# A position bias table fetched in four groups of heads, and a sigmoid that changes places in the last feed-forward

## The reference

```python
rel = kj - BLOCK - qi
bias = rel_bias[t5_bucket(rel)].astype(jnp.float32)
bias = jnp.transpose(bias, (2, 0, 1)).reshape(N_KV_HEADS, G, 1, BLOCK, 3 * BLOCK)
...
scores = jnp.where(valid, scores + bias, NEG_INF)
```

```python
u = causal_dwconv(h2 @ w_up[l], conv_w[l], conv_b[l])
a, v = jnp.split(u, 2, axis=-1)
x = x + gt2 * ((jax.nn.silu(a) * v) @ w_down[l])
```

## Time and profile before

| | |
|---|---|
| median of 3 runs | 1354.23 us (1352.77 to 1354.25) |
| the profiled execution, its own time | 1350.6 us |
| its span, first to last instruction | 1348.8 us |
| PE busy | 1314.8 us |
| DVE busy | 1054.6 us |
| ACT busy | 698.5 us |
| POOL busy | 42.7 us |
| mean granted TensorE clock | 0.995 |
| bytes moved | 262.00 MB, mean 194 GB/s |

### The profile page before, as it was taken

The page is one execution under the profiler, slowest core; times in us unless marked ns, Lnnn a source line. Parts: engine busy times, 40 slices in busy tenths (PEclk is TensorE's granted clock), DMA queues, the critical chain, the costliest instruction groups (busy, mean ns, idle before and its releaser), DMA issues.

```text
span 1348.8 us, 22597 instructions
## 1 busy us (share of the span) xinstructions
PE 1314.8 (97%) x8928; PEld 1197.0 (89%) x8928; DVE 1054.6 (78%) x1814; ACT 698.5 (52%) x1124; POOL 42.7 (3%) x80
## 2 busy tenths in 40 slices
PE   6999999999999999999999999999999998999998
PEld 6999999998888889999999988888879876888886
DVE  4588668786778785787687776788899888688888
ACT  5454554444445454555544354454457566655553
POOL 1000000000000000000000000000010000000000
PEclk9999999999999999999999999999999998999999
DMA  8965435564777654544445745777634504345551
GB/s 264 230 239 185 176 127 217 188 219 157 256 277 285 257 188 157 183 162 156 143 155 220 249 188 199 273 283 290 236 108 172 220 32 145 115 163 207 197 190 61
DMA packets 42147, 262.00 MB, mean 194 GB/s; under 512 B 5229, under 2 KB 5613, under 8 KB 14782
## 3 DMA queue, kind: packets, MB, share of 16 engines
q1 hardware_dynamic: 32688, 227.28, 47.3%
q0 software_dynamic: 9264, 33.24, 7.4%
q10 hardware_dynamic: 94, 0.07, 0.0%
HBM read 258.99 MB, written 1.58 MB: 193 GB/s over the span
## 4 chain that ended last, share of the span: by engine, by line
PE 82%; DVE 10%; DMA 4%; ACT 2%; issue 1%; SPq 0%; DVEq 0%; ACTq 0%
PE psum L726 21%; PE psum L746 15%; PE psum L843 11%; PE psum L732 11%; PE psum L752 8%; PE psum L791 4%; DMA ring<-stream 3%; DVE split L1811 3%; PE psum L798 2%; PE psum L817 2%; PE psum L903 1%; PE psum L893 1%; PE psum L881 1%; DVE arena L1804 1%; PE psum L1012 1%
## 5 line engine op out<-in xcount | busy, mean ns | idle before, releaser
L1811 DVE TENSOR_TENSOR split<-ring,split 128x1024 fp32r<-128x1024 f32 x406 | 480.0, 1220 | 77.4 <-ACT split L1320 76.1
L1320 ACT CAST split<-ring 128x1024 fp32r<-128x1024 f32 x405 | 405.7, 1049 | 170.1 <-PE psum L732 74.4
L726 PE MATMUL psum<-h,split 128*128 128x256 f32 x2176 | 273.4, 283 | 1.0 <-ACT split L1320 1.0
L726 PEld LDWEIGHTS psum<-h,split 128*128 128x128 f32 x2176 | 265.7, 192 | 2.7 <-issue 1.9
L746 PE MATMUL psum<-h,split 128*128 128x512 f32 x960 | 229.0, 390 | 0.7 <-ACT split L1320 0.7
L746 PEld LDWEIGHTS psum<-h,split 128*128 128x128 f32 x960 | 177.7, 188 | 36.4 <-DVE arena L2632 1.1
L843 PE MATMUL psum<-split,feed 128*128 128x512 f32 x792 | 186.1, 391 | 1.3 <-DVE feed L1811 0.7
L843 PEld LDWEIGHTS psum<-split,feed 128*128 128x128 f32 x792 | 146.6, 188 | 31.7 <-DVE split L1811 1.5
L732 PE MATMUL psum<-h,split 128*128 128x256 f32 x1088 | 142.0, 283 | 0.2 <-DVE split L1811 0.2
L732 PEld LDWEIGHTS psum<-h,split 128*128 128x128 f32 x1088 | 135.6, 192 | 0.4 <-DVE split L1811 0.4
L752 PEld LDWEIGHTS psum<-h,split 128*128 128x128 f32 x960 | 123.3, 191 | 4.8
(11 more groups left out here) (328 smaller groups left out, 1389.2 us busy)
## 6 DMA issues: line engine op xcount, KB each, us to landing
ring<-stream SPq DMA_DIRECT2D x213, 1024.0 KB, 4.9
arena<-ada POOLq DMA_DIRECT2D x48, 512.0 KB, 5.3
arena<-bias_by_distance POOLq DMA_DIRECT2D x8, 384.0 KB, 29.7
gain<-norm_rows POOLq DMA_DIRECT2D x4, 512.0 KB, 6.3
x<-x_in SPq DMA_DIRECT2D x2, 512.0 KB, 4.8
ring<-stream SPq DMA_DIRECT2D x2, 512.0 KB, 7.2
gain<-mod_rows POOLq DMA_DIRECT2D x2, 512.0 KB, 4.1
out<-x SPq DMA_DIRECT2D x4, 256.0 KB, 2.0
```

Of the source, the lines that this page charges most:

```text
L726: pe.matmul(to[m], w[0][:, at + k, cols[m]], rhs[:, part, at + k, :], start=m == parts[0] and k + part == 0, stop=False)
L1320: act.copy(split_of(x)[:, 0, n], ring[:, AT[x] % RING, n]).then_inc(wh_ready, 1)
L1811: return dve.tensor_tensor(out_, value, high.bitcast(F32), ALU.subtract)
```

## The change

The bias fetch is cut into four groups of four heads, each of eight transfers of 96 KB, with a semaphore of its own. Group 0 is issued where all was issued before. Group 1 waits until (kd, 1) is done, group 2 until (c, 1) is done, `c_row` as before until (c, 2) is done, group 3 until (x, 3) is done, and the tables of the second block until (wa, 1) is done, which also holds back `gain`. `softmax_in` waits in layer 0 for the group of its heads. In the last feed-forward the sigmoid moves out of fa's turn into fv's, behind fv's copy and the high part that follows it, ahead of fv's first tap. The last down does for the first 128 tokens the high products of both column halves first, and then the low products of each; the other 128 tokens as before.

```diff
+BIAS_HEADS = 4
...
-        bias_in = sem("bias_in")
+        bias_in = [sem(f"bias_in{g}") for g in range(H1 // BIAS_HEADS)]
...
-            for q0 in range(0, P, SHIFTS):
-                pool.dma_start(bias_t[q0:q0 + SHIFTS], bass.AP(bias_dram.tensor, P - 1 - q0, [
-                    [SKEW, SHIFTS], [SHIFTS * (SKEW + 1), H1], [1, 3 * P]])).then_inc(bias_in, 16)
-
-            pool.wait_ge(bias_in, 16 * (P // SHIFTS))
+
+            def bias_group(g):
+
+                heads, row = slice(BIAS_HEADS * g, BIAS_HEADS * (g + 1)), SHIFTS * (SKEW + 1)
+                for q0 in range(0, P, SHIFTS):
+                    pool.dma_start(bias_t[q0:q0 + SHIFTS, heads], bass.AP(bias_dram.tensor, BIAS_HEADS * g * row + P - 1 - q0, [
+                        [SKEW, SHIFTS], [row, BIAS_HEADS], [1, 3 * P]])).then_inc(bias_in[g], 16)
+
+            bias_group(0)
+            pool.wait_ge(job_done, JOB["c", 0])
+            bias_group(1)
+            pool.wait_ge(job_done, JOB["x", 1])
+            bias_group(2)
             pool.wait_ge(job_done, JOB["x", 2])
             pool.dma_start(c_row, c_in.partition_broadcast(P)).then_inc(c_loaded, 16)
+            pool.wait_ge(job_done, JOB["b", 3])
+            bias_group(3)
+            pool.wait_ge(job_done, JOB["ga", 2])
             pool.dma_start(pos_sb[:, :], positions.rearrange("a (n p) -> p (a n)", p=P),
...
-            def down(c, j, parts=(0, 1), ks=range(2), halves_=range(2)):
+            def down(c, j, parts=(0, 1), ks=range(2), halves_=range(2), weights=(0, 1)):
...
-                each(0, False)
-                return each(1, True)
+                for which in weights:
+                    mm = each(which, which == 1)
+                return mm
...
-            for i in range(NT):
-                for a in range(2):
-                    down((L, "down", FJ - 1), FJ - 1, (i,), halves_=(a,)).then_inc(down_used, 1)
+            last = (L, "down", FJ - 1)
+            for a in range(2):
+                down(last, FJ - 1, (0,), halves_=(a,), weights=(0,))
+            for a in range(2):
+                down(last, FJ - 1, (0,), halves_=(a,), weights=(1,)).then_inc(down_used, 1)
+            for a in range(2):
+                down(last, FJ - 1, (1,), halves_=(a,)).then_inc(down_used, 1)
...
                 next_high((L, name, j))
+                if name == "fv":
+                    act.wait_ge(fa_read, 2 * j + 1)
+                    act.activation(fy[:, 2], fy[:, 0], ACT.Sigmoid).then_inc(fsig, 1)
                 act.wait_ge(pair_read, 2 * j + half + 1)
...
                 e.then_inc(fa_lin, 1)
-                if name == "fa":
-                    act.wait_ge(fa_read, 2 * j + 1)
-                    act.activation(fy[:, 2], fy[:, 0], ACT.Sigmoid).then_inc(fsig, 1)
...
                     if i == 0:
-                        dve.wait_ge(bias_in, 16 * (P // SHIFTS))
                         dve.wait_ge(small_loaded, 32)
+                    if l == 0:
+                        dve.wait_ge(bias_in[2 * p // BIAS_HEADS], 16 * (P // SHIFTS))
```

## The result

| | before | changed |
|---|---|---|
| median | 1354.24 us (4 runs, 1352.77 to 1355.57) | 1345.93 us (4 runs, 1344.57 to 1347.20) |
| ratio | | 0.9940, 95% interval 0.9928 to 0.9952 |
| profiled execution, its own time | 1350.6 us | 1346.13 us |
| its span | 1348.8 us | 1344.3 us |

The changed kernel is faster, by 8.3 us in this comparison, where 3.05 us were forecast and 1349.4 us was the lower end of the range. The two profiles differ by only 4.5 us. So there are two questions: what the 4.5 us are, and why the runs differ by more than the profiles.

A forecast was written before the change was run, and what follows sets the result against it. PE was taken as the bound, busy 1314.8 of 1348.8 us, except at the end. Gains of 2.05 us at the start and 1.0 us at the end, together 3.05 us off 1354.23, gave 1351.2 us; range 1349.4 to 1353.3 us.

The forecast's parts named there:

- The gap at the start: PE between 60 and 80 us: three gaps caused by late chunks go with the bias in groups; gain 2.05 us, bounds 0 and 2.05.
- The times of `scores(1)`: Start: DVE's `softmax_in(0)` done at about 76.1 us, PE comes at 77.4 us, so in time by 1.3 us.
- The chunks' rate: Beside a bias group chunks get 0.175 MB per us, PE uses 0.181; they fall behind under half a microsecond in 13 us.
- Why the groups help: Start: group 0 ends at about 33 to 35 us, then chunks have the engines for themselves; ACT's 15.2 us of waiting goes.
- rival D: Start: groups 1, 2 and 3 each bring the stall back, three stalls of 2.05 us; 1357.3 us, chance 0.04.
- Rivals A: Start: the reload collides with group 1, the 1.25 us before `scores(1)` stays; 1352.4 us, chance 0.10.
- B: End gives nothing: DVE waits for fv's first tap, or PE's low products still wait; 1352.2 us, chance 0.09.
- C: Start: chunks are late from start-up traffic, not the bias, so only the end is won; 1353.2 us, chance 0.07.
- The sigmoid: Last feed-forward: moving it is worth nothing up to j = 8, and brings fv 10's taps 2.1 us earlier.
- The last down: End: PE finds `feed` ready, DVE's first quarter starts at 1339.9 instead of 1340.90 us; gain 1.0 us, bounds 0 and 2.1.
- DVE's 2.1 us: End: fv 10's taps and all behind them come 0.58 + 1.17 + 0.33 = 2.1 us earlier; only 1.0 is used.
- The median: Whole kernel: the 3.05 us gain was taken off the runs' median, 1354.23 us, not the profiled 1350.6 us; 1351.2 us forecast.

The follow-up runs named there:

- e5: Changed kernel, but all four bias groups issued at once at the start, late tables where they were; 1346.98 us, ratio 0.9954 to the kernel before.
- e9: e5 with eight heads in a group: two groups issued at once at the start; 1346.58 us, ratio 0.9958 to the kernel before.
- e6: Changed kernel with two groups of eight heads, the second behind (c, 1); 1347.20 us, ratio 0.9958 to the kernel before.
- e7: Changed kernel with the last down in its old order; 1346.09 us, -6.5 +- 1.2 us by means against the kernel before.
- e12: Same kernel as e7, run beside e11 on one chip; 1346.33 us, -6.2 +- 1.1 us by means against the kernel before.
- e4: Changed kernel again, unchanged, for a second profile and the scatter; 1348.11 us, ratio 0.9966 to the kernel before.
- e11: Changed kernel once more, beside its variants on one chip; 1347.29 us, ratio 0.9962, -5.4 +- 1.3 us by means against the kernel before.
- e1: Kernel before, unchanged, for a second profile and the scatter; 1353.79 us, ratio 0.9997 to the kernel before.
- e3: Changed kernel with the bias groups undone and tables where they were, only the end changed; 1352.81 us, ratio 0.9996 to the kernel before.

## Why the prediction was wrong

It had the direction, the likeliest mechanism and its places right, and the size wrong; the measured time lay below the range. By its own steps:

**The gap at the start.** The step that failed is this: "Gain 2.05 us; the bounds are 0 and 2.05, since PE has no more idle time there. I take 2.05 us." The mechanism held (no wait for a chunk, no gap, `scores(1)` in time: DVE's `softmax_in(0)` began at 73.03 us and PE came at 74.61). The size failed twice. The brackets understate a stall; from start to start the same profile had 2.77 us. And one execution was taken for the kernel. The rows with a full queue and a landing time of 24.2 us against some 19 us in hand said that the lag had crossed a threshold; beyond it the three profiles have stalls of 2.77, 4.72 and 4.33 us at 0.152, 0.141 and 0.136 MB per us for the chunks. Measured for this term: 3.94 us over three profiles, 4.15 +- 1.1 us by runs. The upper bound was no bound at all. The times of `scores(1)` held better: PE came 0.7 us behind the end of `softmax_in(0)`'s reading (73.91 us), where 1.3 us was forecast.

**The chunks' rate.** I worked with 0.175 MB per us, an average over 20 to 72 us that includes the last 8 us, in which the bias had nearly run out. While both queues were full it was 0.152 MB per us in this profile, against 0.182 needed. With that figure the ring's loss would have been five times what I had for a group.

**Why the groups help.** I put it down to the fetch being spread over time, and did not see that a transfer of four heads takes less from the chunks while it runs. The size alone is enough (e5, and for PE even e9). Whether late fetching alone is enough was not tested: no run fetches all 16 heads in one transfer and part of them late. With eight heads in a transfer it removed what the size had left, ACT's 8.7 us of waiting (e6 beside e9). The Trainium skill's page that I cited for rival D has the rule; I used it for the danger and not for the gain.

**Rival D.** The groups beside the ring brought no stall: chunks beside group 1 landed in 5.0 to 7.9 us. Rivals A, B and C were wrong as well.

**The sigmoid.** "As long as PE is the bound (j up to 8) this is worth nothing" was wrong at j = 1, by 0.95 us. The wait stands in PE's list of waits for the second block (0.7 us, once), the only one there on ACT's high part, and I had read PE as full from the stretches after 1200 us.

**The last down.** 1.0 us forecast, 1.17 measured, and its 0.91 us for the four products ahead of the first quarter is the 0.90 us of e7 and e12. The size was right, and so was DVE's 2.1 us. But I booked the 1.0 us as the gain of the new order, while the sigmoid's move alone gives 2.07 us there (14.61 to 12.54) and the new order takes 0.90 of it back; the forecast had that loss in its own sum and did not draw the conclusion.

**The median.** I subtracted from the median of the runs a gain read in one profile that was itself 3.6 us faster than that median. That difference was the sign: 1 to 2 us of it is the stall, which was short there.

The terms with their measured sizes: 3.94 + 0.95 + 1.17 = 6.06 us, beside 5.4 to 5.7 us in three comparisons and 8.3 us in the first. They account for the three; the 2.2 us more of the first have no cause in any run.

## What to carry to other kernels

Price a stall from the start of one instruction to the start of the next, over the whole affected stretch and against an unaffected stretch of the same work; the idle time ahead of an instruction is too small. If a profiled execution is faster than the median by more than the effect looked for, take a second profile before a bound is drawn from it. A queue that loses ground slowly against a fixed reserve costs nothing at first, and then a stall that here differed from execution to execution; there a small change of its rate, here by smaller transfers on the other queue, was worth as much as moving most of the other transfers away as well.

## What the runs showed of the hardware

The granted clock of PE differs between executions of one kernel in two stretches of the second block where PE has many short gaps, and some 3 us of the time go with it. The changed kernel twice, e4 and then e11, from 980 to 1000 and from 1080 to 1140 us (PE, PEld, DVE, ACT, POOL busy; then granted clock, DMA share, GB/s):

```profile
980.00:1000.00 20.00, 17.27 (x75) 13.46 (x74) 18.07 (x37) 11.23 (x23) 2.23 (x5) 0.91 0.09 23
...
1080.00:1140.00 60.00, 52.21 (x372) 43.02 (x370) 47.23 (x133) 36.08 (x84) 0.00 (x0) 0.89 0.21 73
```

```profile
980.00:1000.00 20.00, 16.82 (x78) 12.64 (x77) 18.39 (x39) 11.51 (x24) 1.63 (x5) 1.00 0.07 18
...
1080.00:1140.00 60.00, 50.54 (x384) 41.81 (x382) 49.70 (x136) 38.39 (x87) 0.00 (x0) 0.97 0.25 88
```

e4 was ahead by 1.01 us at job (c, 0) (51.83 against 52.84 us) and behind by 2.52 us at down 8 (1325.02 against 1322.50 us), with the same instructions between: 3.5 us. The granted clock of a stretch is a mean of the two levels, 2.4 GHz (1.00) and 1.2 GHz (0.50): from 1105 to 1110 us it was 0.66 in e4 and 1.00 in e11, and there one run of eight products took 1.95 us in e4 and 1.13 in e11. Both kinds of kernel have both kinds of execution (the old fetch has 0.91 and 0.89 in e1, 1.00 and 0.97 in e3). A difference of two single profiles of this kernel is therefore worth nothing below some 3 us, unless it is read stretch by stretch.
